# Down projections with eight of 22 slices as block products, and four sums on GpSimd

## The reference

```
def swiglu(x, w_gu, w_down):
    g, u = jnp.split(x @ w_gu, 2, axis=-1)
    return (jax.nn.silu(g) * u) @ w_down

def trunk_layer(x, ...):
    f1 = swiglu(rmsnorm(x, norm_ffn1_pre), w_ffn1_gu, w_ffn1_down)
    x = x + 0.5 * rmsnorm(f1, norm_ffn1_post)
    mix, state = mixer(rmsnorm(x, norm_mix_pre), ...)   # one wide projection, mLSTM and latent attention, w_out
    x = x + rmsnorm(mix, norm_mix_post)
    f2 = swiglu(rmsnorm(x, norm_ffn2_pre), w_ffn2_gu, w_ffn2_down)
    x = x + 0.5 * rmsnorm(f2, norm_ffn2_post)
```

## Time and profile before

| | |
|---|---|
| median of 3 runs | 1366.59 us (1361.54 to 1367.52) |
| the profiled execution | 1366.81 us, its span 1364.8 us |
| TensorE busy | 97% of the span, 11729 matmuls |
| VectorE, ScalarE, GpSimd busy | 64%, 42%, 11% |
| first down stage | TensorE from 253.5 to 385.9 us |
| second down stage | TensorE from 1218.0 to 1350.6 us |

### The profile page before, as it was taken

The page is one execution under the profiler, slowest core; times in us unless marked ns, Lnnn a source line. Parts: engine busy times, 40 slices in busy tenths (PEclk is TensorE's granted clock), DMA queues, the critical chain, the costliest instruction groups (busy, mean ns, idle before and its releaser), DMA issues. The chain is left out here.

```text
span 1364.8 us, 30387 instructions
## 1 busy us (share of the span) xinstructions
PE 1329.4 (97%) x11729; PEld 1247.5 (91%) x11729; DVE 874.6 (64%) x1689; ACT 566.9 (42%) x1064; POOL 145.1 (11%) x275
## 2 busy tenths in 40 slices
PE   8999999999999999999999999999899999999996
PEld 8999999999989978888789888869899999999995
DVE  5998899822277544554553566664899999983225
ACT  5455555722254334444352332233554555463221
POOL 0000000000003105555551000000000000000000
PEclk9999999999999999999999999979999999999998
DMA  4232233322245627777776133314252223332221
GB/s 161 92 124 93 94 105 125 129 86 85 93 158 189 214 85 218 240 212 219 204 224 246 48 124 142 125 48 157 80 189 94 93 96 119 123 112 98 87 83 66
DMA packets 81075, 180.20 MB, mean 132 GB/s; under 512 B 12137, under 2 KB 46954, under 8 KB 79146
## 3 DMA queue, kind: packets, MB, share of 16 engines
q1 hardware_dynamic: 72746, 161.56, 34.6%
q0 software_dynamic: 8192, 16.79, 4.3%
HBM read 162.01 MB, written 16.30 MB: 131 GB/s over the span
## 5 line engine op out<-in xcount | busy, mean ns | idle before, releaser
L921 PE MATMUL acc<-x_forms,pair_w 128*128 128x272 f32 x1728 | 273.1, 288 | 0.0
L921 PEld LDWEIGHTS acc<-x_forms,pair_w 128*128 128x128 f32 x1728 | 244.2, 188 | 0.0
L2029 DVE TENSOR_TENSOR w_lo<-w_raw,w_hi 128x1024 fp32r<-128x1024 f32 (+1 forms) x92 | 125.4, 1363 | 126.5 <-ACT w_hi L1435 126.5
L998 PE MATMUL acc<-x_hi,w_hi 128*128 128x272 f32 x656 | 199.5, 304 | 0.0
L998 PE MATMUL acc<-x_hi,w_lo 128*128 128x272 f32 x656 | 191.8, 292 | 0.0
L998 PE MATMUL acc<-x_lo,w_hi 128*128 128x272 f32 x656 | 191.6, 292 | 0.0
L1435 ACT ACTIVATE w_hi<-w_raw 128x1024 fp32r<-128x1024 f32 (+1 forms) x92 | 107.5, 1169 | 143.6 <-PE acc L740 79.7
L450 POOL DMA_DIRECT2D pg<-in_lat x256 | 138.3, 540 | 200.1 <-issue 134.7
L998 PEld LDWEIGHTS acc<-x_hi,w_hi 128*128 128x128 f32 x656 | 123.6, 188 | 9.5 <-issue 7.9
L998 PEld LDWEIGHTS acc<-x_lo,w_hi 128*128 128x128 f32 x656 | 123.7, 188 | 5.2 <-issue 4.7
L740 PE MATMUL acc<-h_hi,w_hi 128*128 128x272 f32 x616 | 127.2, 288 | 0.0
(11 more groups left out here) (394 smaller groups left out, 2535.4 us busy)
## 6 DMA issues: line engine op xcount, KB each, us to landing
w_pair<-in_w_gu SPq DMA_DIRECT2D x68, 512.0 KB, 4.2
pg<-in_key_t SPq DMA_DIRECT2D x256, 96.0 KB, 2.5
w_raw<-in_w_dn SPq DMA_DIRECT2D x32, 704.0 KB, 4.1
w_raw<-in_w_in SPq DMA_DIRECT2D x44, 512.0 KB, 4.4
pg<-in_lat POOLq DMA_DIRECT2D x256, 64.0 KB, 2.8
w_raw<-in_w_gu SPq DMA_DIRECT2D x20, 512.0 KB, 3.8
x_mid<-x SPq DMA_DIRECT2D x2, 2176.0 KB, 7.1
g_mid<-sq SPq DMA_DIRECT2D x16, 272.0 KB, 3.4
```

What stands on the lines that cost most here:

```text
L921: ins = nc.tensor.matmul(bank, w[:, k * P:(k + 1) * P], v[:, k, :], start=start and k == 0 and term == 0, stop=k == KD // 2 - 1 and term == 2,
L998: ins = nc.tensor.matmul(acc[0][:, a, 0:HT], w[:, i % 2, k * P:(k + 1) * P], v[:, k, a * HT:(a + 1) * HT], start=k == 0 and term == 0, sto ...
L2029: nc.vector.tensor_tensor(wlo[:, slot, 0:tiles * P], raw[:, slot, 0:tiles * P], f32(whi[:, slot, 0:tiles * P]), ALU.subtract).then_inc(w_s ...
```

## The change

KC = 14 of the 22 slices stay as they are (7 of each unit, `DIRECT`). The other eight, 7 to 10 and 18 to 21, become a 2 x 2 block product for each of four pairs of output tiles: (two tiles) x (two groups of 4 slices) x (two halves of the tokens), seven products of 12 matmuls each. Their parts lie where other things were: the weight blocks in the part of the unit slots that a shorter unit leaves free, in the second half of x and in the places of w4; the forms of h over `xhi` and over `gt` and `sg`. So the forms of h can only be made when all pair products are done and all of h is there. The second half of x is loaded late in the stage, behind product S2 of the last pair.

The low and high parts of seven forms of h (each 128 x 1088) are new once a stage, those of seven weight blocks (128 x 512) once a pair. Of the sums, GpSimd makes S1 and S3 of h and S1 and S3 of each pair's weights; VectorE makes the other two of each. Bank contents are combined by `take` in seven additions a pair. In the last pair, units 14 and 15 are done for half 0 ahead of the products and for half 1 after them. `add_half` is now called for two tiles, not one. The loops are written out.

```diff
+KC = KF - KD
-                           ("dn1", 2 * KD, 11, KD)
+                           ("dn1", 2 * KD, KC // 2, 1)
 # SP
+            def down_stage(name, q):
+                for p in range(4):
+                    weight_units(name, 4 * p, 2)
+                    if p:
+                        sp.wait_ge(dn_used, 7 * (4 * q + p))
+                    else:
+                        sp.wait_ge(pair_split, 7 * (NP * (q + 1) - 1))
+                    for i, n in enumerate((A11, A12, S4, A22)):
+                        sp.dma_start(block_raw[n][:], weights[name][4 * p + i][:, HALF_C * P:]).then_inc(dn_raw, 16)
+                    if p == 0:
+                        sp.wait_ge(pair_used, 7 * NP * (q + 1))
+                        sp.dma_start(x[:, 0:KD // 2, :], (x_mid if q else xT)[:, 0:KD // 2, :]).then_inc(x_again, 16)
+                    weight_units(name, 4 * p + 2, 2)
+                sp.wait_ge(dn_used, used_of(q, 3, S2))
+                sp.dma_start(x[:, KD // 2:KD, :], (x_mid if q else xT)[:, KD // 2:KD, :]).then_inc(x_again2, 16)
 # TensorE
+                for p in range(4):
+                    last = p == 3
+                    if p:
+                        pe.wait_ge(dn_taken, taken_of(q, p - 1, "y12"))
+                    for i in range(2):
+                        direct(4 * p + i, (0, 1), i == 0).then_inc(w_used, 1)
+                    if p:
+                        pe.wait_ge(dn_taken, taken_of(q, p - 1, "y21"))
+                    for i in range(2):
+                        ins = direct(4 * p + 2 + i, (0,) if last else (0, 1), i == 0)
...
+                    for n in (LAST if last else NORMAL):
+                        product(p, n)
+                pe.wait_ge(dn_taken, taken_of(q, 3, "y21"))
+                direct(14, (1,), False).then_inc(w_used, 1)
+                pe.wait_ge(dn_taken, taken_of(q, 3, "y11"))
+                direct(15, (1,), False).then_inc(w_used, 1)
 # ScalarE, the last pair of the gate stage, and the start of the down stage
-                        hi_part(u0 + NC, 0, 11)
-                        for k in range(6):
+                        hi_part(u0 + NC, 0, KC // 2)
+                        for k in range(8):
                             split_h_hi(q, k)
...
+                act.wait_ge(pair_used, 7 * NP * (q + 1))
+                form_hi(A11)
+                form_hi(S1)
+                unit_hi(2)
+                form_hi(S2)
+                form_hi(A12)
+                block_hi_part(0, A11)
+                unit_hi(3)
...
 # VectorE, the same two places, and a pair
-                for k in range(2, 6):
+                for k in range(2, 8):
                     split_h_lo(q, k)
                 take(s, 3)
                 take(s, 4)
                 product(KF - 1, NP * (q + 1))
-                for k in range(6, 11):
+                for k in range(8, 11):
                     split_h_lo(q, k)
-                lo_part(u0 + NC + 1, 1, 11)
-                for k in range(11, KF):
+                lo_part(u0 + NC + 1, 1, KC // 2)
+                for k in range(11, KC):
                     split_h_lo(q, k)
...
+                unit_lo(2)
+                form(0)
+                form(1)
+                form_lo(A11)
+                unit_lo(3)
+                block_sums(0)
+                for n in NORMAL:
+                    if n != A11:
+                        form_lo(n)
+                    block_lo_part(0, n)
+                    if n == S3:
+                        take(0, "part")
+                unit_lo(4)
+                for what in TAKE_NORMAL[1:]:
+                    take(0, what)
+                    if what == "y11":
+                        unit_lo(5)
+                for p in range(1, 4):
+                    sums(2 * p - 2)
+                    sums(2 * p - 1)
+                    unit_lo(4 * p + 2)
+                    block_sums(p)
+                    for n in NORMAL:
+                        block_lo_part(p, n)
+                        if n == S2:
+                            unit_lo(4 * p + 3)
+                    if p < 3:
+                        unit_lo(4 * p + 4)
...
                     if a == 0 and k == KD - 2:
+                        add_half("f2post", KD - 2, 1)
                         add_half("f2post", KD - 1, 1)
 # GpSimd
+            def down_sums(q):
+                pool.wait_ge(h_full, KF * (q + 1))
+                pool.wait_ge(pair_used, 7 * NP * (q + 1))
+                for n, a, b in ((S1, b12, b11), (S3, b22, b12)):
+                    nc.gpsimd.tensor_tensor(h_form(n)[2], a, b, ALU.subtract).then_inc(hf_sum, 1)
+                for p in range(4):
+                    pool.wait_ge(dn_raw, 64 * (4 * q + p + 1))
+                    r = block_raw
+                    nc.gpsimd.tensor_tensor(r[S1][:], r[S4][:], r[A22][:], ALU.add).then_inc(dn_sum, 1)
+                    nc.gpsimd.tensor_tensor(r[S3][:], r[A11][:], r[S4][:], ALU.subtract).then_inc(dn_sum, 1)
```

More of the change, by code:

```diff
@@ new lines, in layer, with h_form @@
+        FIRST_K, SECOND_K = slice(HALF_C, KF // 2), slice(KF // 2 + HALF_C, KF)
+        DN_STAGE = dict(dn1=0, dn2=1)
+        DN_NORM = dict(dn1="f1post", dn2="f2post")
+        NORMAL, LAST = [A11, S1, S2, A12, S4, S3, A22], [A11, S1, S2, S4, S3, A22, A12]
+        HI_FIRST = [A11, A12, A22, S1, S2, S4, S3]
+        TAKE_NORMAL = ["part", "y11", "y12", "pg", "tq", "y22", "y21"]
+        TAKE_LAST = ["part", "y12", "pg", "y22", "tq", "y21", "y11"]
+        def h_form(n):
+            cols = HALF[0] if n in (S4, A22) else HALF[1]
+            if n in (S1, S2):
+                i = 0 if n == S1 else 2
+                return hf[:, i, :, :], hf[:, i + 1, :, :], hf_raw[:, i + 1, :, :]
+            if n == S3:
+                return h3[:, 0, :, :], h3[:, 1, :, :], h3_raw[:, 1, :, :]
+            k = FIRST_K if n in (A11, A22) else SECOND_K
+            return hhi[:, k, cols], hlo[:, k, cols], hid[:, k, cols]
@@ L969, in _ @@
             gate_stage("gu1", "f1pre")
-            down("dn1", 0)
+            down("dn1")
             def turn_values(i):
@@ new lines, in take @@
+                def take(p, what):
+                    y0, y1 = 2 * p, 2 * p + 1
+                    late = A.bank(f"{norm}1")[:, 0:HT]
+                    c21 = acc[1][:, 1, 0:HT]
+                    out, bank, add, n = {
+                        "part": (part_, acc[2][:, 1, 0:HT], q_, S1),
+                        "y11": (y_ffn[:, y0, HALF[1]], acc[0][:, 1, 0:HT], kept_, A12),
+                        "y12": (y_ffn[:, y0, HALF[0]], acc[0][:, 0, 0:HT], part_, S4),
+                        "pg": (pg_, late, part_, S3), "tq": (tq_, late, q_, S3),
+                        "y22": (y_ffn[:, y1, HALF[0]], acc[1][:, 0, 0:HT], pg_, S3),
+                        "y21": (c21 if p == 3 else y_ffn[:, y1, HALF[1]], c21, tq_, A22)}[what]
+                    dve.wait_ge(dn_used, used_of(q, p, n))
+                    if what == "part":
+                        dve.wait_ge(dn_kept, 2 * (4 * q + p) + 2)
+                    if taken_of(q, p, what) > 1:
+                        dve.wait_ge(dn_taken, taken_of(q, p, what) - 1)
+                    nc.vector.tensor_tensor(out, bank, add, ALU.add).then_inc(dn_taken, 1)
@@ new lines, in down @@
+                unit_lo(4)
[12 more added lines that the diff above has]
+                            unit_lo(4 * p + 3)
+                    if p < 3:
+                        unit_lo(4 * p + 4)
+                    for what in (TAKE_NORMAL if p < 3 else TAKE_LAST[:6]):
+                        take(p, what)
+                        if what == "y11" and p < 3:
+                            unit_lo(4 * p + 5)
@@ L2346, in _ @@
+                add_half(norm, KD - 2, 0)
+                add_half(norm, KD - 1, 0)
+                take(3, "y11")
+                if name == "dn1":
+                    lo_of_first("in", 0)
+                dve.wait_ge(dn_taken, 28 * (q + 1))
             dve.wait_ge(setup, 1)
```

260 lines of the change are left out of this document (197 added, 63 removed).

## The result

The changed kernel takes 1380.66 us (median of 5 runs, 1379.38 to 1382.54) against 1365.60 (5 runs): ratio 1.0115, 95% interval 1.0094 to 1.0136. It is slower; the forecast was 1364.0, range 1360 to 1371. The profiled execution spans 1377.8 us for 1364.8 before.

The account below looks back on a forecast made before the run. TensorE, 97% busy, was taken to bound the kernel except at the down stages' ends. Savings of 2 x 2.5 less stalls of 2 x 0.95 less 0.4 gave 2.7 us less: 1364 us, 80% range 1360 to 1371.

Parts of the forecast that it names:

- Step 5: GpSimd's sums at a stage's start: 1.1 to 5.5 us per 1088-element difference; at most the second 0.9 late.
- step 4: Start of a stage, TensorE catching the splits: stalls of 0.95 us a stage, three meetings with under 0.1 of room.
- The first meeting: Start of a stage: TensorE reaches unit 1 before its low part is split and stalls 0.8 us.
- Rival (a): Stage starts: VectorE's operations double beside GpSimd, 6.3 us instead of 0.95 a stage, 1374.6; chance 0.20, half at about 1369.
- Step 1: Matmuls taken away: 48 fewer a stage, 5.5 us, or 11 for both stages if the same things ended last.
- Steps 2 and 3: Second and first stage ends: each gains 2.5 us ahead of s (half 0 sum); second add costs 0.4, transfers 0.
- rival (e): Clock may fall while TensorE idles at the first stage's end: 0 to 2 us; chance 0.04 with a smaller stall.
- Step 6: Pairs 1 to 3: transfers and splits arrive in time, cost 0, with 2.1 and 0.3 us of room.
- (b): Stage start: first large GpSimd operation late by a one-time cost; if 8.4 us, 1366.6; chance 0.05.
- (c): Transfers: 1472 KB take 9 us instead of 6.3, six pairs stall 0.6 each, first end adds 2: 1369.5; chance 0.13.
- (d): Full saving shows because VectorE chains behind s (half 0 sum) hide less than counted: 1355.5 to 1359; chance 0.06.

Follow-up runs that it names:

- e2_vector_sums: The changed kernel with all of GpSimd's sums and differences moved to VectorE; 1377.51 us, ratio 1.0111.
- e3_pool_late: The changed kernel with GpSimd's first difference waiting until all 14 direct slices of h are split; 1374.22 us, ratio 1.0081.
- e1_probe: The kernel before with unneeded GpSimd work added: a memset and four two-input operations in the first stage, a memset and four copies in the second; 1375.75 us, ratio 1.0088.
- e11_order: e10_middle_vector with the sixth unit's low part moved up in VectorE's queue, behind the second form's low part; 1356.68 us, ratio 0.9938.
- e9_middle: The changed kernel with block products only in the second and third pair, first and last plain, weights' sums on GpSimd; 1362.71 us, ratio 0.9982.
- e13_pieces: The changed kernel with each GpSimd sum and difference cut into four instructions over a quarter of the columns; 1373.46 us, ratio 1.0063.
- e12_order_pool: e11_order with the two weight sums of each pair on GpSimd again; 1359.42 us, ratio 0.9958.
- e10_middle_vector: e9_middle with the two weight sums of each pair on VectorE instead of GpSimd; 1362.12 us, ratio 0.9979.
- e6_head: e2_vector_sums with unit 1 split ahead of slices 8 to 10; 1377.39 us, ratio 1.0086.
- e7_tail: e6_head with the last pair's A12 product moved behind unit 14's half 1 matmuls; 1382.71 us, ratio 1.0125.

## Why the prediction was wrong

The four columns came out 14.9 us longer where the steps said 2.7 less: 17.6 to explain. 8.7 of it lie in stage 1 (132.36 - 125.17, and 1.55 for the forecast's 2.5 less 0.95), 7.3 in stage 2, 0.8 at the first end, 0.8 at the second.

- **Step 5 failed, and took step 4's stalls with it.** It asked how long GpSimd's operations take and when their results are wanted, and priced their effect on VectorE at nothing. Their length was inside the bounds: 2.56 for 1088 elements, 1.30 for 512 alone, and the estimate of 2.4 by the Trainium skill (GPSIMD Engine Reference, 3.1) was near; the 4 ns per element of the upper bound stood in no row, measured are 2.2 ((2.55 - 1.30) / 576). But each of VectorE's operations waits for the rest of one of them: the three slices took 4.65 more and unit 1's low part 1.06, 5.7 in all, on top of the 0.56 that e2_vector_sums has at this place. With 6.23 of wait, 2.7 of clock and 0.65 in the last pair, the first stage lost some 9.7 (7.2 and the 2.5 saved) for the forecast's 0.95; the second, with 6.23, 1.6 and 0.43, lost 8.3.
- **Step 4, the size without GpSimd.** The first meeting held: with VectorE undisturbed unit 1 is 0.56 late (e2_vector_sums, e3_pool_late), forecast 0.8. For the rest no run shows the step's own case. All sums on VectorE cost 5.1 of waits a stage (e2_vector_sums), with two forms and two sums a pair more to make; all on GpSimd but later, 3.5 and 4.3 (e3_pool_late). Neither is near 0.95, and the step's own remark, that three meetings had under 0.1 us of room, was the better reading.
- **Rival (a) was the right mechanism, mis-sized.** Doubling gave 6.3 a stage and a chance of 0.20 (its three delays, 3, 0.8 and 1.9, added to the 0.95 make 6.65, a slip of 0.35 a stage). The row "against it", the `add_half` beside a memset, was no evidence: a memset reads nothing, as the text itself said, and in e1_probe VectorE runs freely beside one and is held up by a copy. The clock behind the wait was in no case of (a).
- **Step 1 held**: 96 matmuls less at their pace; e11_order shows 2.8 to 3.0 us a stage for 24.
- **Steps 2 and 3 held in kind.** What follows s didn't shorten with TensorE's work: s to the first of the late adds is 8.72 (1363.77 - 1355.05), 8.69 before. The first norm step came at s + 2.96, forecast s + 3.05, behind the units' low parts as forecast, and TensorE was let on at s + 8.11. Mis-sized: the second add 0.57, taken as 0.4, and at both ends the clock, which TensorE met after idling: 0.8 at the first (rival (e) had 0 to 2), and 0.55 at the second, where the sum behind 5.40 of idle takes 1.27 (clock 0.50 from 1364 to 1366; 0.73 in e9_middle behind 1.82).
- **Step 6 held but for the last pair**: 64 us of middle pairs without a gap; 0.65 and 0.43 at the last pair's second one-sided unit, where 0.3 of room was counted. The term that was short is the transfer: the pair's first unit is there 7.0 us behind the first issue (355.96 to 362.95), counted 6.3, and the splits behind it took about as long as counted (6.7 for 6.5).
- **Rivals (b), (c) and (d) fell as causes of the loss**: the first GpSimd difference took 2.56, and 2.55 in the second stage; the whole saving showed nowhere. The sign of (c) did show, landings later than 6.5 us, but it cost only the 0.65 and 0.43 of the last pairs; TensorE waited for no transfer itself.

That order and place in the stage decide is shown (e9_middle to e12_order_pool); that GpSimd's whole instructions, for which VectorE waits, cause the 6.23 is shown by e1_probe, e2_vector_sums (0.56 without them) and e13_pieces (2.46 with short ones). Left open: what the stage's start would cost with GpSimd's sums and no lock, which can't be run, and why the clock falls in some executions and not in others.

## What to carry to other kernels

Work isn't moved from VectorE to GpSimd for free: before it is, list the VectorE operations of two SBUF inputs that run beside it, and add to each the rest of a whole GpSimd instruction; where the engine behind is on the path, keep GpSimd off that stretch or cut its instructions short. In this kernel a saving of matmuls was worth its count only where the splitting engines have slack: take it in the middle of a stage, and leave the start (where everything is being split) and what stands behind the last sum as they are. In an in-order queue, put first what is wanted first: one line moved (e10_middle_vector to e11_order, 3.7 us in the columns) gave back more than moving the sums between engines did (2.7 from e9_middle to e10_middle_vector). And before a profiled execution is compared with another, compare their granted clocks outside the part that was changed.

## What the runs showed of the hardware

- VectorE's two-input operations and GpSimd's instructions that read SBUF, copies included, take turns whole: VectorE ends 0.58 or 0.59 us after GpSimd's end for 544 elements, whatever GpSimd's instruction is (differences of 1088 and 272 elements, sums of 512, a copy of 1088). A memset doesn't hold it up (0.73 and 0.72). GpSimd loses too: 2.99 for 2.55, 1.75 for 1.30.
- GpSimd: 1.30 us for a two-input operation on 128x512, 2.56 on 128x1088, 0.77 or 0.78 on 128x272 (e13_pieces, 255.04 and 255.77); a copy of 128x1088 1.14, begun beside the end of a slice, and of 128x512 0.99, both in e1_probe.
- After 6.2 us of idle TensorE ran at a granted clock of 0.50, the 1.2 GHz level, for about 6 us of full work. After 1.5 (e2_vector_sums) it stayed at 1.00. After 1.8 at the same place of the first stage it stayed at 1.00 in e6_head and fell in e7_tail (0.69 from 264 to 268); after 2.5 it was 1.00 in e13_pieces' first stage and fell in its second (0.60 from 1232 to 1236). So for waits of about 2 us the length alone doesn't tell.
